# One expert step of a fused transformer block started from rows of four token tiles, the fifth tile's rows added by 0/1 products

## The reference

```python
p_grp = jax.nn.softmax(x32 @ wg + bg, axis=-1)
g_sel = jnp.argmax(p_grp, axis=-1)
fine_sel = fine[:, g_sel, :]                      # 8 experts of the chosen group
top_v, top_i = lax.top_k(fine_sel, 2)
combine = jnp.sum(one_hot(expert_idx, 32) * w_fine[..., None], axis=1)
act = jax.nn.silu(x @ w_gate[e]) * (x @ w_up[e]) * combine[:, e, None]
y = sum_e act @ w_down[e]
```

## Time and profile before

| | us |
|---|---|
| median of 3 runs (lowest, highest) | 621.42 (620.03, 621.8) |
| the profiled execution | 620.28 |
| its span, first to last instruction | 618.4 |
| PE busy | 585.6 (95%) |
| DVE busy | 350.7 (57%) |
| ACT busy | 179.5 (29%) |
| POOL busy | 101.0 (16%) |

### The profile page before, as it was taken

One profiled execution on the slowest core, in us unless ns is written; L12 is line 12 of the kernel. 1 busy time (PEld: TensorE's weight loads), 2 busy tenths in 40 slices (PEclk: granted clock), 3 DMA queues, 4 the chain that ended last, 5 costly groups with the idle time before them and its releaser, 6 DMA issues.

```text
span 618.4 us, 9365 instructions
## 1 busy us (share of the span) xinstructions
PE 585.6 (95%) x3274; PEld 325.9 (53%) x3275; DVE 350.7 (57%) x781; ACT 179.5 (29%) x375; POOL 101.0 (16%) x134
## 2 busy tenths in 40 slices
PE   5899999999998999999999979999999999987995
PEld 2443555555565676645554536555555555554452
DVE  2745898755565888654666884333433333332367
ACT  4203787701145777731111101111111111110110
POOL 4000011121233000000000111222212121211222
PEclk9999999999999999999999999999999999997999
DMA  8999833430028739539113979999999999999996
GB/s 323 376 376 355 317 146 149 178 136 2 0 81 248 293 91 268 244 110 401 69 69 126 357 247 361 420 417 417 419 416 417 417 422 419 419 418 418 400 384 252
DMA packets 47922, 175.95 MB, mean 284 GB/s; under 512 B 11556, under 2 KB 17712, under 8 KB 34320
## 3 DMA queue, kind: packets, MB, share of 16 engines
q1 hardware_dynamic: 36240, 154.60, 64.4%
q0 software_dynamic: 6688, 15.48, 7.2%
q10 hardware_dynamic: 4960, 5.42, 2.5%
HBM read 163.11 MB, written 21.14 MB: 298 GB/s over the span
## 4 chain that ended last, share of the span: by engine, by line
PE 76%; DMA 13%; SPq 4%; DVE 4%; issue 2%; ACTq 1%; ACT 0%; DVEq 0%; POOL 0%; POOLq 0%
PE ps L1809 18%; PE ps L1622 11%; PE ps L1535 9%; PE ps L1547 8%; PE ps L1827 8%; DMA expert_w<-exp_w_up 5%; PE ps L1662 4%; PE ps L1689 4%; DMA gate_w<-lru_wx 3%; PE ps L1510 3%; PE ps L1671 3%; PE ps L1775 2%; SPq L370 2%; PE ps L1456 2%; DMA recurrence<-w_mod 2%
## 5 line engine op out<-in xcount | busy, mean ns | idle before, releaser
L1809 PE MATMUL ps<-expert_w,hT_mixT 128*64 128x256 f32 x1120 | 136.5, 394 | 5.9 <-DMA expert_w<-exp_w_up 5.4
L1809 PEld LDWEIGHTS ps<-expert_w,hT_mixT 128*64 128x64 f32 x1120 | 85.0, 137 | 61.1 <-issue 17.9
L1535 PE MATMUL ps<-hT_mixT,w 128*128 128x128 f32 (+1 forms) x256 | 72.6, 437 | 1.2 <-DVE hT_mixT L958 1.2
L1622 PE MATMUL ps<-w,hT_mixT 128*128 128x512 f32 x160 | 71.9, 597 | 0.0
L1827 PE MATMUL ps<-expert_w,hT_mixT 128*64 128x512 f32 x276 | 65.8, 599 | 0.0
L774 ACT ACTIVATE hT_mixT<-ps 128x128 f32<-128x128 f32 x36 | 10.0, 277 | 187.4 <-PE ps L1809 187.4
L1535 PEld LDWEIGHTS ps<-hT_mixT,w 128*128 128x128 f32 x256 | 38.9, 191 | 35.8 <-issue 32.6
L1353 DVE SCALAR_TENSOR_TENSOR hT_mixT<-hT_mixT,ps 128x128 f32<-128x128 f32 x36 | 10.4, 288 | 80.0 <-ACT hT_mixT L774 80.0
L1547 PE MATMUL ps<-w_qkv,hT_mixT 128*128 128x512 f32 (+1 forms) x160 | 53.1, 488 | 0.0
L1371 DVE TENSOR_TENSOR w<-ps,w 128x1024 f32<-128x1024 f32 x17 | 20.8, 1224 | 56.5 <-PE ps L1827 56.5
L1622 PEld LDWEIGHTS ps<-w,hT_mixT 128*128 128x128 f32 x160 | 29.1, 191 | 29.8 <-issue 29.6
(11 more groups left out here) (295 smaller groups left out, 762.0 us busy)
## 6 DMA issues: line engine op xcount, KB each, us to landing
expert_w<-exp_w_down SPq DMA_DIRECT2D x30, 1024.0 KB, 18.2
expert_w<-exp_w_gate SPq DMA_DIRECT2D x29, 1024.0 KB, 14.5
expert_w<-exp_w_up SPq DMA_DIRECT2D x29, 1024.0 KB, 16.6
w_mod_ring<-w_mod SPq DMA_DIRECT2D x14, 1024.0 KB, 6.5
y_rows<-zero_rows POOLq DMA_DIRECT2D x10, 512.0 KB, 6.0
expert_w<-y_rows SPq DMA_DIRECT2D x10, 512.0 KB, 7.9
recurrence<-w_mod SPq DMA_DIRECT2D x8, 512.0 KB, 9.9
w<-w_in SPq DMA_DIRECT2D x4, 1024.0 KB, 16.6
```

Source lines behind the costliest of these rows:

```text
L1535: ins = pe.matmul(ps[:, bank, 0:n], w1v[:, c, m * P:(m + 1) * P], HM[:, c, lo:lo + n], start=(c == 0), stop=(c == DC - 1))
L1622: ins = pe.matmul(ps[:, 2 * (t % 2) + half, :], HM[:, c, t * P:(t + 1) * P], w1v[:, c, half * 512:(half + 1) * 512], start=(c == 0), stop= ...
L1809: ins = pe.matmul(ps[r, 2 + k, 0:2 * P].rearrange("p (k f) -> p k f", k=2), xT[:, c, r], gate_up(i)[:, :, c, k:FF:FC], start=(c == 0), sto ...
```

## The change

Step 0 is taken apart. Its rows of tiles 0 to 3 are found, by the table `hit0`, as soon as tile 3 has its slots: 8 products of one column follow the last projection, and ACT writes the 128 indices to `idxc`. POOL gathers these rows (bounds 512) without waiting for tile 4's h2. PE multiplies the gathered rows by the identity, and adds `h2_last` times `first_slot`, a 0/1 matrix of tile 4's tokens by step 0's slots, into the same PSUM banks; these had been started by two products with a `first_slot` of zeros, which stand for two of the products that nobody reads. Ranks and slots now count from 1. ACT copies both halves of `xT`.

The steps of the pairs (`last`, `first`, `final`) are written before tile 4's tokens get their steps. Step 0 starts when `last` is there; after its first 16 gate products, PE does the 10 products that give `tid` of all steps, and after its down the 20 products for the weights. The gather for step 1 waits for that `tid` and `last_rows`; the gather for step 2 is issued before the loop, and so is step 0's scatter. The rows' weight moves from the activation (L1356) to the eviction (`y_evict`). SP loads the down weights of expert 5 and a half of a kept one before `h2` of tile 4, and expert 5's gate right after it. POOL's clearing of `xg` stands before the end of tile 4's norm.

```diff
@@ SP, the loads before the first refill
+            sp.wait_ge(S["x1T_v"], NT)
+            w_down(sp, 5, 5)
+            sp.dma_start(W1[:, 6 * D:7 * D], wd_v[KEPT, :, 0:D]).then_inc(kept_in, 16)
             sp.wait_ge(S["h2"], NT)
             sp.wait_ge(S["lg_mm"], NT)
-            sp.dma_start(W1[:, 6 * D:7 * D], wd_v[KEPT, :, 0:D]).then_inc(kept_in, 16)
+            sp.dma_start(ring[:, HOME[5], 0:EW], wg_v[5]).then_inc(wgu_in[2], 16)
             sp.dma_start(kept_down[1], wd_v[KEPT, :, D:2 * D].rearrange("p (c n) -> p c n", c=DC)).then_inc(kept_in, 16)
             sp.wait_ge(last_rows, 16)
+            sp.wait_ge(S["xt_mm"], 3)
             sp.dma_start(W1[:, 5 * D:6 * D], wd_v[member(KEPT_HALF, 0), :, 0:D]).then_inc(kept_in, 16)
-            sp.wait_ge(S["xg_in"], 16)
-            sp.dma_start(ring[:, HOME[5], 0:EW], wg_v[5]).then_inc(wgu_in[2], 16)
-            w_down(sp, 5, 5)
             sp.wait_ge(S["route_ok"], 3)
@@ ACT
             x1_out(NT - 1, 0)
+            act.wait_ge(S["idx_mm"], 1)
+            act.activation(idxc[:, :], ps[:, 2, 0:1], ACT.Copy, bias=float(TOK)).then_inc(S["tid_ok"], 1)
             squares_2(NT - 1, 1)
             x1_out(NT - 1, 1)
             h2_out(NT - 1)
+            for half, done in enumerate((S["xT_v"], S["xT_a"])):
+                act.wait_ge(S["xt_mm"], 2 + half)
+                act.activation(xT[:, 4 * half:4 * half + 4, :], ps[:, half, :].rearrange("p (c n) -> p c n", c=4), ACT.Copy)\
+                   .then_inc(done, 1)
@@ POOL
-            pool.wait_ge(last_rows, 16)
             pool.wait_ge(S["tid_ok"], 1)
...
-            gather(tid[:, 0:1])
+            gather(idxc[:, 0:1], rows=LAT)
             pool.wait_ge(S["xt_mm"], 1)
+            pool.wait_ge(last_rows, 16)
+            pool.wait_ge(S["tid_ok"], 2)
             gather(tid[:, 1:2])
+            pool.wait_ge(S["xt_mm"], 4)
+            gather(tid[:, 2:3])
             pool.wait_ge(S["route_ok"], 4)
-            end = every_step_but_last(pool, step_of)
+            pool.wait_ge(S["y_out"], 16)
+            pool.wait_ge(S["y_v"], 2)
+            scatter(pid[:, 0:1])
+            end = every_step_but_last(pool, step_of, since=1)
@@ DVE, after h2 of the last tile
-            follow(last_tile)
...
+            ranked(last_tile)
+            step(dve.tensor_reduce(first_rank, prod[:, :, 0:2], AX, ALU.add))
+            step(dve.scalar_tensor_tensor(out=first_place, in0=first_rank, scalar=SLOTS + 0.625, in1=first_rank,
+                                          op0=ALU.is_lt, op1=ALU.mult))
+            step(dve.tensor_scalar(first_slot, col["slot"], first_place[:, 0:1], None, ALU.is_equal))
+            dve.scalar_tensor_tensor(out=first_slot, in0=col["slot"], scalar=first_place[:, 1:2], in1=first_slot,
+                                     op0=ALU.is_equal, op1=ALU.add).then_inc(S["slot"], 1)
...
+            dve.tensor_copy(last[:, :], start[:, 1:1 + PAIRS]).then_inc(S["route_ok"], 1)
+            dve.tensor_copy(first[:, :], start[:, 0:PAIRS]).then_inc(S["route_ok"], 1)
+            dve.tensor_scalar(final[:, :], start[:, PAIRS:PAIRS + 1], -1.0, None, ALU.add).then_inc(S["route_ok"], 1)
+            follow(last_tile)
@@ DVE, a step
-                dve.scalar_tensor_tensor(out=act2[:, c, :], in0=sg[:, c, :], scalar=now[:, 0:1], in1=ps[:, 2 + c, P:2 * P],
-                                         op0=ALU.mult, op1=ALU.mult).then_inc(S["act_ok"], 1)
+                dve.tensor_tensor(act2[:, c, :], sg[:, c, :], ps[:, 2 + c, P:2 * P], ALU.mult).then_inc(S["act_ok"], 1)
...
-                dve.tensor_tensor(y, wide[:, 5 * 512:5 * 512 + D], gsel, ALU.mult).then_inc(S["y_v"], 1)
+                dve.scalar_tensor_tensor(out=y, in0=wide[:, 5 * 512:5 * 512 + D], scalar=now[:, 0:1], in1=gsel,
+                                         op0=ALU.mult, op1=ALU.mult).then_inc(S["y_v"], 1)
@@ PE
+            slot_tokens(ps[:, 2, 0:1], LT, hit0.unsqueeze(3))
             x1_turn(NT - 1, 1)
             logits(NT - 1)
...
-            keep_clock(4)
+            keep_clock(3)
...
+            for half in range(2):
+                pe.matmul(ps[:, half, :], first_slot, ring[:, HOME[0], 0:512], start=True, stop=False)
             rank(NT - 1)
-            keep_clock(4)
-            pe.wait_ge(S["slot"], TOP * NT + 1)
...
-            keep_clock(5)
+            pe.wait_ge(S["xg_in"], 16)
+            for c in range(DC):
+                ins = pe.matmul(ps[:, c // 4, (c % 4) * P:(c % 4 + 1) * P], xg[:, c:D:DC], ident[:, :], start=False, stop=False)
+            ins.then_inc(S["xt_mm"], 1)
+            pe.wait_ge(S["h2"], NT)
+            pe.wait_ge(S["slot"], TOP * LT + 2)
+            for c in range(DC):
+                ins = pe.matmul(ps[:, c // 4, (c % 4) * P:(c % 4 + 1) * P], h2_last_flat[:, c:D:DC], first_slot, start=False, stop=(c % 4 == 3))
+                if c % 4 == 3:
+                    ins.then_inc(S["xt_mm"], 1)
...
+                        elif routing and k == 0:
+                            pe.wait_ge(S["slot"], TOP * NT + 3)
+                            pe.wait_ge(S["y_v"], n + 1)
+                            slot_tokens(ps[:, 4, 2 * P:2 * P + COLS], NT, hit)
```

More of the change, by code:

```diff
@@ L351, in every_step, with every_step_but_last @@
             return steps
-        def every_step_but_last(e, body):
+        def every_step_but_last(e, body, since=0):
             end = e.value_load(final[0:1, 0:1])
-            with e.Fori(0, end) as n:
+            with e.Fori(since, end) as n:
                 body(n)
@@ L1250, in slots @@
                 dve.wait_ge(S["rank_rd"], t + 1)
+            def slots(t):
                 step(dve.tensor_reduce(ranks, prod, AX, ALU.add))
-                step(dve.tensor_scalar(block_f, ranks, 0.5 - SLOTS / 2, 1.0 / SLOTS, ALU.add, ALU.mult))
+                step(dve.tensor_scalar(block_f, ranks, -0.5 - SLOTS / 2, 1.0 / SLOTS, ALU.add, ALU.mult))
                 step(dve.tensor_scalar(blockno[:, t, :], block_f, ROUND, ROUND, ALU.add, ALU.subtract))
@@ L1332, in _ @@
                .then_inc(S["stepw"], 1)
-            dve.wait_ge(S["tid_ok"], 1)
-            dve.wait_ge(last_rows, 16)
+            dve.wait_ge(S["tid_ok"], 2)
             step(dve.tensor_copy(info[:, :, 2], tid[:, :]))
             step(dve.tensor_scalar(info[:, :, 1], info[:, :, 2], float(LAT), None, ALU.is_ge))
-            x_out(0)
-            dve.wait_ge(S["w_mm"], 1)
-            step(dve.tensor_copy(moved, ps[:, 5, 0:COLS]))
-            step(dve.tensor_tensor(info[:, :, 0], moved, ps[:, 5, COLS:2 * COLS], ALU.add))
@@ new lines, in _ @@
+            step(dve.tensor_copy(moved, ps[:, 7, P:P + COLS]))
+            step(dve.tensor_tensor(info[:, :, 0], moved, ps[:, 7, P + COLS:P + 2 * COLS], ALU.add))
+            step(dve.tensor_tensor(info[:, :, 0], info[:, :, 0], ps[:, 7, P + 2 * COLS:P + 3 * COLS], ALU.add))
+            dve.wait_ge(S["idx_mm"], 3)
+            step(dve.tensor_scalar(moved, ps[:, 4, P:P + COLS], float(TOK), None, ALU.add))
+            dve.tensor_tensor(pid[:, :], moved, info[:, :, 2], ALU.add).then_inc(S["route_ok"], 1)
@@ L1378, in step_of @@
                 y_evict(n)
-            end = every_step_but_last(dve, step_of)
+            row_facts(0)
+            y_evict(0)
+            end = every_step_but_last(dve, step_of, since=1)
             def base(t):
@@ L1757, in keep_clock, with slot_tokens @@
                     pe.matmul(ps[:, 3, :], ident[:, :], ring[:, HOME[0], 0:512], start=True, stop=True)
+            def slot_tokens(out, tiles, steps):
+                for t in range(tiles):
+                    for k in range(TOP):
+                        ins = pe.matmul(out, slotp[:, t, k, :], steps[:, t, k, :],
+                                        start=(t == 0 and k == 0), stop=(t == tiles - 1 and k == TOP - 1))
+                ins.then_inc(S["idx_mm"], 1)
+            pe.wait_ge(S["slot"], TOP * LT + 1)
+            pe.wait_ge(S["gated"], 2 * LT - 1)
+            slot_tokens(ps[:, 2, 0:1], LT, hit0.unsqueeze(3))
             x1_turn(NT - 1, 1)
@@ L1850, in visits @@
                     step_of(n, s, visit, kept, kept_half)
-            for s in range(HELD):
+            pe.wait_ge(S["route_ok"], 1)
+            hi = pe.value_load(last[0:1, 0:1])
+            with pe.Fori(0, hi) as n:
+                step_of(n, 0, 1, routing=True)
+            pe.wait_ge(S["route_ok"], 3)
+            for s in range(1, HELD):
                 visits(s, s, 1)
```

133 lines of the change are left out of this document (70 added, 63 removed).

## The result

The change makes the kernel slower: 626.38 us in the median of five runs (625.13 to 627.49) against 621.42, a ratio of 1.0087 with a 95% interval of 1.0071 to 1.0103. Forecast were 616.7 us, range 611.0 to 622.0. The profiled execution took 626.11 us, its span 624.2.

The account below looks back on a forecast made before the run. PE was taken to set the time of steps 0 to 13, the weight stream that of step 15. 620.28 - 3.7 (stream) - 1.0 (clock) = 615.6 profiled, 1.1 below the median: 616.7 us, range 611.0 to 622.0.

Parts of the forecast that it names:

- to step 1: Time from the start of the projection's last six products to the start of step 1; the forecast had 35.3 us.
- Two sets of 8 real products, each 1.7 us as the logits' 8 are: PE before step 0: products of gathered and tile 4's rows replace 8 transposes of 0.89 us; step 0 starts at 365.3.
- The gathers, 7.6 and 7.2 us: Landing times taken for the gathers of step 0 (rows there at 360.6) and step 1 (at 375.9).
- SP's queue is thin for a moment: At step 1's gather, issued at 368.7: the reason to take 7.2 us, between 7.6 and 3.8.
- The wait inside step 0, 2.9 us: PE, done with gate and up at 373.0, waits for step 1's gather; PE gains 1.6 us of the 5.3.
- Neither wait is as long as 4.6: Argument against the clock falling at PE's two gather waits: the longer earlier wait for weights was 4.6 us.
- the third rival: Clock falls at both gather waits, step 1 4.4 us later than before (about 387), 623.7 us; chance 0.12.
- Every refill waits for PE ... 2.1 us of other work stood there.: Weight stream at the thinnest refill, 476 us: stream gains at most PE's 1.6 plus 2.1, so 3.7 us.
- The loads fill gaps, a gain.: DMA from 344 to 380 us: 6.1 us of idle time to win; first refill at 369.3 instead of 374.50.
- The end.: Step 15 starts 3.7 us sooner, 1.0 us counted for the clock in its gate and up, tail unchanged.

Follow-up runs that it names:

- e9: Changed kernel with weight tiles of 128 adjacent columns instead of every eighth one in both sets of step 0's real products; 623.97 us, ratio 1.0048.
- e10: Changed kernel with the ten products for the slots' tokens moved from behind the first 16 gate products to between the sets; 620.98 us, ratio 0.9995.
- e3: Changed kernel with four unread products before the wait for step 1's gather, within step 0; 625.12 us, ratio 1.0060.
- e17: e9 with four unread products in the wait for step 1's gather, as in e3; 621.08 us, ratio 1.0005.
- e5: Kernel before the change with only the new order of SP's last weight loads; 626.19 us, ratio 1.0085.
- e12: Changed kernel with the edits of e9 and e10 together; 617.44 us, ratio 0.9958.
- e18: e10 with four unread products in front of the wait for step 0's gather; 621.02 us, ratio 1.0012.
- e2: Changed kernel with four unread products before the wait for step 0's gather only; 627.58 us, ratio 1.0105.
- e4: Changed kernel with SP's loads before the first refill in the order of the kernel before; 624.51 us, ratio 1.0064.
- e7: Changed kernel with the two sets exchanged, tile 4's products in front of the wait for step 0's gather; 625.61 us, ratio 1.0076.
- e15: e10 with SP's loads in the order of the kernel before; 621.43 us, ratio 1.0014.
- e1: Changed kernel with four unread products before each of the waits for the gathers of steps 0 and 1; 624.77 us, ratio 1.0074.
- e11: Changed kernel with the edits of e7 and e10 together; 618.32 us, ratio 0.9951.
- e13: e11 with the gathered rows transposed into banks of their own and added by DVE, instead of real products; 617.72 us, ratio 0.9939.
- e14: e13 with SP's loads in the order of the kernel before; 618.11 us, ratio 0.9951.

## Why the prediction was wrong

Step 1 was to start at 381.5 and started at 389.59, 8.1 us later (7.3 by "to step 1": 42.6 for 35.3). By the prediction's own steps:

- **"Two sets of 8 real products, each 1.7 us as the logits' 8 are": 3.95 each, +4.4** (the 4.19 and 3.72 of the chain, forecast 3.5). This is the step that failed first. I took a price from a row of the same form, 128x128 float32 weights, and did not look at how the tiles lie in memory. e9 shows it: 192 ns a weight load for 336, by the layout alone. But with this put right (e9) the time is still 624.0, 7 above the forecast; the next points are the larger part.
- **The gathers, 7.6 and 7.2 us: 8.20 and 8.21.** With its issue gather 0 came 0.9 late, gather 1 another 1.0. "SP's queue is thin for a moment" was true, the DMA share was 0.16 from 372 to 376, and no help: SP issued four refill loads from 374.56 on, 0.8 us behind the gather. By the Trainium skill (DMA: Bandwidth & Descriptors, Anatomy of one DMA), 2.0 us plus the bytes at 436 GB/s, an estimate of 2.3 us for 35 rows and 2.6 for 66, both would have been hidden; the trace does not agree, with 8.20 and 8.21.
- **The wait inside step 0, 2.9 us: 3.58.** That there would be one was right; its price was taken as its length alone, and this is the second step that failed. e10, which removes the wait, gains 5.4 us. The wait also decides the clock of what follows: transposes 1.97 us for 1.05, down 4.12 for 3.65, +1.4. The last 20 products with the start of step 1 took 1.4 for 0.9, +0.5. With the 4.4 and 1.9 above this makes 8.2; smaller ones are left that nearly cancel (the copies behind the sets took 0.7 for 1.2; the gather for step 1 left 3.6 us behind step 0's start for 3.4).
- **The clock.** "Neither wait is as long as 4.6" was the argument against the third rival. Two waits of 3.6 us brought it down. The rival's own marks came true: step 1 beyond 387 (389.59), time 626.1 for its 623.7. It was given 0.12. That is no merit of its sum, which had sets of 1.7 us and 2.1 us of slack in the stream. In the changed kernel the clock was the smaller part: 1.4 us behind the second wait (in e3 step 1 comes 1.5 us sooner), next to nothing in the dear sets. It costs 3 us where the sets are cheap (e9, e17).
- **"Every refill waits for PE ... 2.1 us of other work stood there."** Fed with step 1's true start this gives 6.5 - 2.1 = 4.4 us; step 15 was 5.95 late. From step 1 to step 15 it took 176.5 us, before 177.0: the slack was 0.5, not 2.1. Right in kind, and it makes the time follow step 1's start. The forecast (381.5 and 556.4) needs 174.9 us between the two; no profiled execution has under 175.8, and in e5, e9 and e10, which start step 1 4.8, 3.7 and 2.5 us late, step 15 is 4.9, 2.5 and 1.2 late. PE's waits for weights were to shrink to 3.3 us and stayed at 5.5.
- **The loads fill gaps, a gain.** The 24th slice is fuller, and the first refill was not sooner (374.56 for 374.50), since PE was not. e5 shows the order's other side, the store and the gather that then stand behind weights. I had the row for it, the store of 5.97 us on the chain, and read it as gone.
- **The end.** Gate and up of step 15 took 9.00 for 10.24 us, the 1.0 counted there. The tail from there on is 1.1 longer (last scatter 8.73 for 7.81 us). 620.28 + 5.95 - 1.24 + 1.1 = 626.1, the profiled time.

The nearest to the forecast's number is e12, 617.44 for 616.7, and that is luck: e12 has no wait for gather 1, and the forecast had paid 2.9 us for one. Without it, by its own steps, step 1 would start at 378.6, the stream gain 6.1 and the time be 614.3, an estimate 3 us below e12. The forecast's own picture, sets of 2 us with gather 1 behind the first quarter of gate and up and no stretch at the low clock behind it, is e17: 621.08, level with the kernel before and 4.4 us above the forecast. The 5.3 us by which step 0 was to start sooner are mostly spent inside step 0; the forecast saw this and priced it too low.

Open: why e18's earlier step 1 did not show in its runs, what keeps e17 4.4 us above the forecast in its median (its profiled execution is its slowest), and why the last scatter takes 0.9 us more.

## What to carry to other kernels

Price a product by a row whose weight tile has the same step in memory, not only the same shape and type. One profiled execution is not the median: read an edit's effect from a fixed point just in front of it, and look at the clock ahead of the edit too. When a wait is moved into a hot stretch, price it with the instructions behind it at the low clock, and look for the few small products (here ten, 0.4 us) whose place decides when the next transfer is issued. When loads are moved forward, list the stores and gathers that then land behind them, and who waits for these.

## What the runs showed of the hardware

- A float32 weight load of 128 columns at a step of 32 bytes lasts 336 ns, against 192 for adjacent ones (after, e9). A set with sixteen of the former takes 3.9 to 4.2 us at either clock (0.50 in the changed kernel, 1.00 in e2), so the low clock cost next to nothing there. With adjacent columns it does cost: the sets took 2.05 and 1.95 us at 1.00 (e9), 3.79 and 2.91 in e17, where the clock was 0.50 to 0.73.
- Eight transposes of the same `xg` at the same step, one weight load of some 192 ns each, overlapping, take 1.05 us; eight real products 3.9, with two loads of 336 ns each. So for weights at this step a real product costs nearly four times a transpose.
- Two indirect gathers landed after 8.2 us, one with the engines full and one with their share at 0.16 when it was issued.
- With bulk loads of weights moved forward, in front of and beside it, a store of 512 KB issued at the same time as before landed after 8.2 us instead of 6.0 (e5).
- The waits of 2.65 to 4.35 us on PE in front of step 1 (in the changed kernel and its repeat, e2, e3, e4, e5, e7, e9, e12, e15, e17) were each followed by a stretch at the low clock; one of 2.37 us in e9 was not. Shorter ones in front of sets with the 32-byte step were followed by it too, one to four us into the sets: 0.9 us in e1, 1.6 in e7, e11, e13 and e14, 2.0 in e10. Whether the sets themselves help to bring the clock down is open; in e2 and e18, where unread products filled the wait, it stayed at 1.00 through the same sets.
